# Four RMS norms hand their factors to the rows through memory instead of through TensorE

## The reference

```python
def rms_norm(x, g, eps=EPS):
    xf = x.astype(jnp.float32)
    y = xf * lax.rsqrt(jnp.mean(xf * xf, axis=-1, keepdims=True) + eps)
    return (y * g.astype(jnp.float32)).astype(x.dtype)

# first_block, shortened
h = h + diff_attention(rms_norm(h, attn_norm_g[0]), ...)
h = h + sq_relu_mlp(rms_norm(h, mlp_norm_g[0]), w_up[0], w_down[0])   # norm 1
hn = rms_norm(h, kv_in_norm_g); ckv = hn @ w_dkv                      # norm 2 (with attn_norm_g[1] too)
c = rms_norm(ckv[..., :256], kv_norm_g)                               # norm 3
cq = rms_norm(hn2 @ w_dq, q_norm_g); q = (cq @ w_uq)                  # norm 4
h = h + mla_attention(...)
h = h + sq_relu_mlp(rms_norm(h, mlp_norm_g[1]), w_up[1], w_down[1])   # norm 5
```

## Time and profile before

| | |
|---|---|
| median of 3 runs | 1815.76 us (1815.21 to 1815.92) |
| profiled execution, its own time | 1815.61 us |
| its span in the trace | 1813.5 us |
| mean granted TensorE clock | 0.999 |
| busy: PE, weight loads, DVE, ACT, POOL | 1799.1, 1462.4, 879.6, 623.7, 536.9 us |
| TensorE's longest wait in the list of waits | 1.1 us |

### The profile page before, as it was taken

One profiled execution on the slowest core, in us unless ns is written; L12 is line 12 of the kernel. 1 busy time (PEld: TensorE's weight loads), 2 busy tenths in 40 slices (PEclk: granted clock), 3 DMA queues, 4 the chain that ended last, 5 costly groups with the idle time before them and its releaser, 6 DMA issues.

```text
span 1813.5 us, 21889 instructions
## 1 busy us (share of the span) xinstructions
PE 1799.1 (99%) x8494; PEld 1462.4 (81%) x8496; DVE 879.6 (48%) x1223; ACT 623.7 (34%) x916; POOL 536.9 (30%) x340
## 2 busy tenths in 40 slices
PE   9999999999999999999999999999999999999999
PEld 8877788888888887788888888877677888888877
DVE  6556563333334767553333334479655422333357
ACT  4344532222222345422222224334645332221244
POOL 1222254132325530153232225423222220210232
PEclk9999999999999999999999999999999999999999
DMA  5322222222322234325222322322122222232222
GB/s 211 108 84 78 75 93 93 93 93 93 104 97 100 79 108 131 111 93 128 93 93 94 114 93 89 115 81 70 55 92 97 93 93 93 93 116 86 100 95 92
DMA packets 37058, 177.70 MB, mean 98 GB/s; under 512 B 4569, under 2 KB 11513, under 8 KB 18041
## 3 DMA queue, kind: packets, MB, share of 16 engines
q1 hardware_dynamic: 35808, 175.06, 28.7%
q10 hardware_dynamic: 1176, 1.63, 0.7%
HBM read 161.99 MB, written 3.67 MB: 91 GB/s over the span
## 4 chain that ended last, share of the span: by engine, by line
PE 88%; DVE 8%; ACT 2%; issue 1%; POOL 1%; DMA 0%; SPq 0%; DVEq 0%; ACTq 0%; POOLq 0%
PE ps L564 23%; PE ps L565 22%; PE ps L566 22%; PE ps L619 3%; PE ps L618 3%; PE ps L596 3%; PE ps L830 1%; PE ps L792 1%; DVE wlo L1751 1%; PE ps L841 1%; DVE idx_score L2223 1%; DVE top L2221 1%; PE ps L638 1%; PE ps L1010 1%; PE ps L1020 1%
## 5 line engine op out<-in xcount | busy, mean ns | idle before, releaser
L1751 DVE TENSOR_TENSOR wlo<-raw,whi 128x2048 fp32r<-128x2048 f32 x133 | 325.8, 2449 | 301.6 <-ACT whi L1249 301.1
L564 PE MATMUL ps<-xb,whi 128*128 128x512 f32 (+1 forms) x996 | 388.4, 390 | 1.4 <-ACT probs L1553 0.8
L566 PE MATMUL ps<-xb,wlo 128*128 128x512 f32 (+1 forms) x996 | 386.1, 388 | 0.0
L565 PE MATMUL ps<-xb,whi 128*128 128x512 f32 (+1 forms) x996 | 386.1, 388 | 0.0
L1249 ACT ACTIVATE whi<-raw 128x2048 fp32r<-128x2048 f32 x143 | 273.0, 1909 | 324.6 <-PE ps L566 248.9
L564 PE MATMUL ps<-xa_hi,whi 128*128 128x512 f32 x788 | 308.5, 391 | 0.7 <-ACT probs L1318 0.7
L566 PE MATMUL ps<-xa_hi,wlo 128*128 128x512 f32 x788 | 306.8, 389 | 0.0
L565 PE MATMUL ps<-xa_lo,whi 128*128 128x512 f32 x788 | 306.7, 389 | 0.0
L564 PEld LDWEIGHTS ps<-xb,whi 128*128 128x128 f32 x996 | 187.1, 188 | 43.6 <-issue 5.0
L566 PEld LDWEIGHTS ps<-xb,wlo 128*128 128x128 f32 x996 | 187.0, 188 | 38.6
L565 PEld LDWEIGHTS ps<-xb,whi 128*128 128x128 f32 x996 | 187.1, 188 | 37.4
(11 more groups left out here) (332 smaller groups left out, 2428.3 us busy)
## 6 DMA issues: line engine op xcount, KB each, us to landing
raw<-wst SPq DMA_DIRECT2D x148, 1024.0 KB, 4.8
stage<-qk_raw SPq DMA_DIRECT2D x32, 128.0 KB, 2.3
mla_qn<-q_nope SPq DMA_DIRECT2D x8, 256.0 KB, 2.4
mla_v<-v_tok SPq DMA_DIRECT2D x8, 256.0 KB, 2.7
outT<-h SPq DMA_DIRECT2D x7, 256.0 KB, 2.0
h<-xT SPq DMA_DIRECT2D x3, 512.0 KB, 7.4
bias_scratch<-bias_rows ACTq DMA_DIRECT2D x1, 1536.0 KB
raw<-wst SPq DMA_DIRECT2D x4, 256.0 KB, 6.0
```

What stands on the lines that cost most here:

```text
L564: pe.matmul(out, lhs_hi, rhs_hi, start=first, stop=False)
L565: pe.matmul(out, lhs_hi, rhs_lo, start=False, stop=False)
L566: return pe.matmul(out, lhs_lo, rhs_hi, start=False, stop=last)
L1751: dve.tensor_tensor(wlo[slot][:, :], raw[slot][:, :], whi[slot][:, :].bitcast(F32), ALU.subtract).then_inc(wlo_done, 1)
```

## The change

For norms 1, 2, 4 and 5 PE's `broadcast` and DVE's copy fall away. POOL, having made `rstd_t`, writes it by a DMA of its own to a row `factors` in device memory (one number at a time, 512 of them), waits until it has landed, and reads that row back to all 128 rows of `rstd_f` by a second DMA. DVE waits for that (`factor_ready`) where it waited for the copy. In `mlp` (norms 1 and 5) the mean is taken ahead of the second `lo` instead of behind it. The other norms are as they were; their counters are renumbered.

```diff
+BY_MEMORY = (1, 2, 4, 5)
+BY_PE = (0, 3, 6, 7, 8, 9, 10, 11)
+COPIED = (0, 3, 6, 7, 9, 11)
...
+        factors = nc.dram_tensor("factors", (len(BY_MEMORY), S), F32, kind="Internal").ap()
...
                     for u in range(4):
-                        hook = None
-                        if first and u == 1:
-                            hook = lambda k: broadcast(norm) if k == 4 else None
-                        elif first and u == 2 and rows:
+                        if first and u == 2 and rows:
                             bias_by_distance()
...
-            features((c + 1) % 2, c + 1, t + 2, xa_hi, xa_lo, hook=lambda k: broadcast(2) if k == 4 else None)
+            features((c + 1) % 2, c + 1, t + 2, xa_hi, xa_lo)
...
-            broadcast(4)
...
             def take_rstd(n, dst=None):
-                dve.wait_ge(bc_done, n + 1)
+                dve.wait_ge(bc_done, BY_PE.index(n) + 1)
                 dve.tensor_copy((rstd_f if dst is None else dst)[:, :], BC[:, :]).then_inc(rstd_f_done, 1)
-                dve.wait_ge(rstd_f_done, n + 1)
+                dve.wait_ge(rstd_f_done, COPIED.index(n) + 1)
+
+            def factor_ready(n):
+                dve.wait_ge(factor_in, 16 * (BY_MEMORY.index(n) + 1))
...
                         if first and u == 0:
+                            mean_square(norm, D)
                             lo(c + 2, c % 2)
-                            mean_square(norm, D)
-                            take_rstd(norm)
+                            factor_ready(norm)
...
             mean_square(2, D)
-            take_rstd(2)
+            factor_ready(2)
...
             lo(c + 2, c % 2)
-            take_rstd(4)
+            factor_ready(4)
...
             def rstd(n):
                 pool.wait_ge(ms_done, n + 1)
                 pool.tensor_tensor(rstd_t[:, 4 * n:4 * n + 4], ms_t[:, 4 * n:4 * n + 4], half_neg[:, :], ALU.pow).then_inc(rstd_t_done, 1)
+                if n in BY_MEMORY:
+                    j = BY_MEMORY.index(n)
+                    pool.wait_ge(rstd_t_done, n + 1)
+                    pool.dma_start(factors[j, :].rearrange("(q p) -> p q", p=P), rstd_t[:, 4 * n:4 * n + 4],
+                                   allow_slow_non_contiguous=True).then_inc(factor_out, 16)
+                    pool.wait_ge(factor_out, 16 * (j + 1))
+                    pool.dma_start(rstd_f[:, :], factors[j:j + 1, :].to_broadcast([P, S])).then_inc(factor_in, 16)
```

More of the change, by code:

```diff
@@ L394, in build @@
         rows_stored = sem("rows_stored")
+        factor_out = sem("factor_out")
+        factor_in = sem("factor_in")
         nbias_full = sem("nbias_full")
@@ L715, in late_rstd, with linear @@
                     stat(norm)
-                elif k == (4 if norm == 0 else 6):
-                    if norm == 0:
-                        pe.wait_ge(const_loaded, 16 * len(consts))
+                elif k == 4:
+                    pe.wait_ge(const_loaded, 16 * len(consts))
                     broadcast(norm)
-            def linear(stage, pairs, xhi, xlo, fresh, norm=None, hook=None):
+            def linear(stage, pairs, xhi, xlo, fresh, hook=None):
                 c, t = C[stage], T[stage]
                 features(c % 2, c, t, xhi, xlo, fresh=fresh, hook=hook)
-                features((c + 1) % 2, c + 1, t + 2, xhi, xlo,
-                         hook=(lambda k: late_rstd(norm, k)) if norm is not None else None)
+                features((c + 1) % 2, c + 1, t + 2, xhi, xlo)
                 with pe.Fori(1, pairs) as i:
@@ L742, in one_round @@
                     for u in range(4):
-                        hook = None
-                        if first and u == 1:
-                            hook = lambda k: broadcast(norm) if k == 4 else None
-                        elif first and u == 2 and rows:
+                        if first and u == 2 and rows:
                             bias_by_distance()
-                        features((c + u) % 2, c + u + 8 * r, t + 2 * u, xhi, xlo, per=16, i=r, hook=hook,
+                        features((c + u) % 2, c + u + 8 * r, t + 2 * u, xhi, xlo, per=16, i=r,
                                  fresh=(xh_done, xl_done, x0) if first and u == 0 else None)
@@ L1070, in final_rstd @@
                 if k == 4:
-                    pe.wait_ge(rstd_f_done, 7)
+                    pe.wait_ge(rstd_f_done, COPIED.index(6) + 1)
                     broadcast(6)
@@ L1677, in take_rstd @@
             def take_rstd(n):
-                act.wait_ge(bc_done, n + 1)
+                act.wait_ge(bc_done, BY_PE.index(n) + 1)
                 act.activation(rstd_f[:, :], BC[:, :], ACT.Copy).then_inc(rstd_f_done, 1)
@@ L2413, in pair @@
                             lo_halves(c + 2, (1,))
-                            dve.wait_ge(rstd_f_done, 9)
+                            dve.wait_ge(rstd_f_done, COPIED.index(9) + 1)
                         tt = t + 2 * s
@@ L2463, in _ @@
             lo_halves(c + 2, (1,))
-            dve.wait_ge(rstd_f_done, 10)
+            dve.wait_ge(rstd_f_done, COPIED.index(11) + 1)
             for u in range(4):
```

## The result

| | median | runs | ratio to before, 95% interval |
|---|---|---|---|
| before, beside it | 1815.49 us | 4 (1814.56 to 1815.92) | |
| with the change | 1845.13 us | 4 (1844.31 to 1845.81) | 1.0164 [1.0146, 1.0181] |

The change costs 29.6 us, and lies far outside the range on record. The spans of the two profiled executions, 1813.5 and 1842.2 us, differ by 28.7; the profiled one of the change is the shortest of its four.

A forecast was written before the change was run, and what follows sets the result against it. PE was taken as the bound, busy 99% of the span with 88% of the chain. Norms 1, 2, 4 and 5 summed -0.89 + 2.3 - 0.91 - 0.89 = -0.4 us: median 1815.4, range 1812.3 to 1820.5.

The forecast's parts named there:

- X: Time from the end of POOL's power to the factor in rstd_f, by write and read: estimated 7.1 us.
- The upper bound of 10.0: High end of X in us: twice the 5.0 of the 48 KB load buckets, queued behind others.
- 1.0 us per DMA: Added to X for POOL making each of the write and the read, 2.0 us in all.
- The rival with a slow first DMA: POOL's first DMA, at norm 1, delayed by Y costs Y - 1.65; slower from Y = 5.7 us; chance 0.07.
- The covers of norms 1 and 5 (8.75, 9.6): X up to these us stays hidden before u=2 in norms 1 and 5; each then gains 0.89 us.
- norm 2's 4.8: Norm 2 isn't free: its ckv is delayed by X - 4.8, 2.3 us at X = 7.1.
- Norm 4's cover: X up to 10.7 us stays hidden before norm 4's rotation; PE gains 0.91 us.
- the slow road: Rival: X over 9.6 makes norms 1, 2 and 5 pay, sum 3X - 25.8, +4.2 us at 10.0; chance 0.16.
- TensorE's clock: Rival: after norm 2's 2.6 us wait PE runs at 1.2 GHz, ending 1 to 3 us over forecast; chance 0.04.
- The mean moved ahead: In norms 1 and 5, mean before DVE's second lo; at norm 1 mean and power end at about 263.2.
- no wait of PE at u=2 of norms 1 and 5: Profile sign of being right; PE waiting for a bank there was named as a sign of being wrong.
- The old wait at `ukv`: PE's 0.18 us wait for DVE's wlo behind norm 2, forecast to grow by some 0.8 us.

The follow-up runs named there:

- experiment 3: The changed kernel with each partition's four factors written as one 16-byte piece, 128 pieces in place of 512, token order left wrong: 1814.1 us.
- experiment 6: Two runs of the changed kernel with written pieces laid out differently, a cosine row read back: single numbers 64 bytes apart 1814.79 us, layout varied by norm 1817.14 us.
- experiment 5: The changed kernel with only norm 4 through memory: 1818.95 us; the kernel before with only the mean moved ahead in norms 1 and 5: 1815.51 us.
- experiment 4: The changed kernel with 84 unused matmuls put into TensorE's three long waits, in norms 1, 2 and 5: 1839.71 us.
- experiment 2: The changed kernel with the DMAs of norms 1, 2 and 5 issued from ACT's queue, norm 4 through TensorE: 1837.77 us.

## Why the prediction was wrong

**The step that failed is X, above all the write's landing in it.** The prediction took 2.7 us for the write, "nearest: `mla_v` also has 512 pieces", and 7.1 for the road. Measured: 8.6 to 10.0 and 14.1 to 16.1. `mla_v`'s 512 pieces are 512 bytes each and go to SBUF; that likeness in number was the wrong one, as experiments 3 and 6 show: what counts is how densely small pieces lie in memory, and no row of before had such a write. The upper bound of 10.0, twice the 5.0 of `buckets`, fell too, since it doubled a transfer of another kind.

**The read and POOL's part.** The prediction added 1.0 us per DMA for POOL. POOL's issues are 0.94 and 0.57 us, but they lie inside the landing times of the DMA view. So the read was taken at 2.4 + 1.0 = 3.4 us and took 4.9 to 5.6, which also goes past the 5.0 of its upper bound; the write was taken at 3.7. The rival with a slow first DMA did not come: norm 1's write, 9.9 us, is like norm 5's, 10.0. Nor did DVE's `wlo` beside it hold POOL up: the issue took 0.94 us there and 0.83 in the three others.

**The covers of norms 1 and 5 (8.75, 9.6) and norm 2's 4.8 held.** With the measured X they give the waits to within 0.1 us or so, and experiment 3 agrees. Norm 4's cover was mis-sized, 10.7 for 12.9: the prediction had its rotation start when its tile is ready, but in the trace of before it starts straight behind DVE's `wlo`, at 671.27:

```profile
669.06 2.29 DVE L1751 TENSOR_TENSOR wlo<-raw,whi 128x2048 fp32r<-128x2048 f32 x1
```

It could have started some 2 us later before TensorE waited for its bank. The clock's 1.6 us hid that. In all the formulas give 25.1 of the 29.5 us. The rival that came true is the slow road, which was priced up to X = 12; at X = 15.4, the mean of the four, its formula 3X - 25.8 and norm 4's X - 10.7 give +25.1.

**TensorE's clock was seen as a rival at 0.04 and 1 to 3 us; it came, with some 6 us.** It is no independent case: it follows from the slow road, and all four waits pay it, not one. Whether it would have come at the forecast's own X, with a wait of 2.6 us in norm 2, no run shows: the clock didn't fall behind norm 2's waits of 1.3 and 1.6 in experiments 3 and 6, and did behind norm 4's waits of 1.7, 1.8 and 2.2 (each with a second, short one close behind).

**The mean moved ahead** was taken at nothing, and measured at +0.1 us (experiment 5); the interval is 0.9992 to 1.001, so up to 1.5 us less or 1.8 us more is not excluded.

**Of what the profile was to show** the missing `broadcast` groups and the two waits from norm 2 were right in kind; "no wait of PE at u=2 of norms 1 and 5" was wrong, and was named as what would make the prediction wrong. The old wait at `ukv`, forecast to grow, is gone: TensorE comes there late itself, after its slow matmuls. Where the clock stays, in experiments 3 and 4, the wait is there, with 0.55 and 0.56 us.

Open stay the length of the stretch in which pieces disturb one another, what holds such a write up behind its packets, and why the read takes now 3.0 (from ACT, norm 2), now 6.7 us: a 1 MB load beside it in norms 1, 4 and 5 is one candidate, but in the changed kernel it took 4.9 in norm 2 too, with no such load. Nor was it tried what norm 2 would need to be covered.

## What to carry to other kernels

A chain of DMAs that a norm or a softmax waits for is judged by each transfer's landing against its own cover, and a landing must be taken from a transfer of the same direction and the same density of pieces; where none is in the trace, the upper bound is open, and the forecast should say so. Write several neighbouring numbers per partition in one piece, or spread single ones 16 bytes apart, and make the order where an engine has time: here POOL's squares, at 0.09 us each, rather than DVE's reads or TensorE's weights. Look at the granted clock behind every new wait of TensorE, short ones too, and add the slow matmuls to its price: here a wait of about 2 us cost 1.6 more. And read the parts of a stretch as well as its sum: a sum that fits can hide two errors.

## What the runs showed of the hardware

- A write of 2 KB to device memory as single numbers next to one another lands after 8.0 to 10.3 us from either queue, and after 2.3 when they are 16 bytes apart or more, with the same number of pieces (experiments 2, 4 and 6).
- While such a write is landing, a 1 MB load runs at 0 to 45 GB/s and takes 12.6 to 13.1 us, against 4.9 beside a write with its numbers 64 bytes apart.
- Reading with a step of 16 bytes costs each engine differently: DVE 1.07 us in place of 0.69, TensorE's `stat` 1.80 in place of 0.95, POOL 1.13 in place of 1.04. The Trainium skill (GPSIMD Engine Reference, Performance pitfalls for Q7 kernels) has a step over 8 bytes cost half as much again per element; this multiply on POOL shows a tenth.
- After waits of 5.1 to 9.4 us (the change, experiment 2) TensorE runs at the lower of its two clock levels, with matmuls 0.43 us apart in place of 0.23, for 2.7 to 4.9 us. Behind norm 4's waits of 1.7 to 2.2 us it does so too, for some 3 us (the change, experiments 4 and 5); behind waits of up to 1.6 us it didn't. Products that nobody reads, put into the three long waits, kept the clock there, and that kernel was 5.4 us faster.
